# The order in which the two feed-forwards stream a product's moving columns: plain, or every 2nd, 4th, 8th or 16th group of 16 columns first

## The reference, cut to what matters

```python
# first block, layers l = 0, 1: widths 1024 -> 4096 -> 1024
f = jnp.square(jax.nn.relu(x @ mlp_w1[l])) @ mlp_w2[l]
x = _layernorm(DEEPNORM_ALPHA * x + f, ln2_g[l], ln2_b[l])

# second block, layers l = 0, 1: widths 1024 -> 2 * 2816, 2816 -> 1024
up = _dwconv(u @ w_up[l], ffn_conv_w[l], ffn_conv_b[l])
a_half, v_half = jnp.split(up, 2, axis=-1)
h = h + (jax.nn.silu(a_half) * v_half) @ w_down[l]
```

## Time and profile before

| what | value |
|---|---|
| median of 3 runs | 2493.92 us (2493.91 to 2503.79) |
| span of the profiled execution, first to last instruction | 2488.1 us |
| TensorE matmul busy | 2442.7 us, 98%, 17296 instructions |
| TensorE weight load busy | 2242.2 us, 90% |
| VectorE, ScalarE, GpSimd busy | 72%, 58%, 12% |
| HBM traffic over the span | 172 GB/s |
| chain that ended last | TensorE 91%, VectorE 6%, ScalarE 2%, DMA 1% |

### The profile page before, as it was taken

How to read it: one execution, slowest core, us unless ns; L and a number is a source line. 1 busy time by engine, 2 the same in 40 slices (tenths; PEclk the granted TensorE clock), 3 DMA queues, 4 the chain that set the end, 5 groups by cost and what they waited for, 6 DMA issues and landing times.

```text
span 2488.1 us, 42214 instructions
## 1 busy us (share of the span) xinstructions
PE 2442.7 (98%) x17296; PEld 2242.2 (90%) x17296; DVE 1787.2 (72%) x2889; ACT 1450.6 (58%) x2130; POOL 287.8 (12%) x222
## 2 busy tenths in 40 slices
PE   8999999999999999899999999999999999999998
PEld 8888999888889899799999799998899999899996
DVE  5567675565586755678778887885598678887875
ACT  5547555445465554477665655664767656656654
POOL 0000002000000000002123720000012207500000
PEclk9999999999999999999999999999999999999999
DMA  7544576655545566554566645666554567645663
GB/s 257 157 138 119 158 248 199 202 180 164 139 118 153 182 191 203 166 156 125 144 199 189 195 139 185 195 202 191 145 153 136 150 194 203 183 146 190 190 210 127
DMA packets 358917, 430.45 MB, mean 173 GB/s; under 512 B 20616, under 2 KB 286310, under 8 KB 358468
## 3 DMA queue, kind: packets, MB, share of 16 engines
q1 hardware_dynamic: 341312, 401.72, 52.9%
q10 hardware_dynamic: 14340, 14.93, 2.5%
q0 software_dynamic: 3072, 11.10, 1.4%
HBM read 424.44 MB, written 3.24 MB: 172 GB/s over the span
## 4 chain that ended last, share of the span: by engine, by line
PE 91%; DVE 6%; ACT 2%; DMA 1%; issue 1%; ACTq 0%; POOL 0%; POOLq 0%; DVEq 0%
PE ps L112 89%; PE ps L115 2%; DVE wlo L121 1%; DVE sE L121 1%; ACT lnv L118 0%; DMA kT<-in_diff_lambda 0%; DVE sbc L130 0%; DVE sE L124 0%; DVE kT L121 0%; DVE sz L130 0%; DMA mxb<-spread 0%; DMA memN<-in_mem 0%; DVE ys L130 0%; DVE xN L130 0%; ACT L118 0%
## 5 line engine op out<-in xcount | busy, mean ns | idle before, releaser
L121 DVE TENSOR_TENSOR wlo<-wring,whi 128x1024 fp32r<-128x1024 f32 (+1 forms) x768 | 919.3, 1217 | 250.6 <-ACT whi L118 249.8
L118 ACT ACTIVATE whi<-wring 128x1024 fp32r<-128x1024 f32 (+1 forms) x768 | 804.0, 1054 | 428.1 <-PE ps L112 414.7
L112 PE MATMUL ps<-uT,whi 128*128 128x256 f32 x4640 | 816.7, 280 | 6.3 <-DVE wlo L121 5.0
L112 PEld LDWEIGHTS ps<-uT,whi 128*128 128x128 f32 x4640 | 704.0, 188 | 14.8 <-DVE wlo L121 8.2
L112 PE MATMUL ps<-uT,wlo 128*128 128x256 f32 x2320 | 645.2, 278 | 0.0
L112 PEld LDWEIGHTS ps<-uT,wlo 128*128 128x128 f32 x2320 | 437.9, 189 | 0.0
L112 PE MATMUL ps<-xT,whi 128*128 128x256 f32 x2112 | 373.9, 281 | 2.9 <-DVE xT L121 1.7
L112 PEld LDWEIGHTS ps<-xT,whi 128*128 128x128 f32 x2112 | 320.5, 188 | 9.3 <-issue 5.6
L112 PE MATMUL ps<-xT,wlo 128*128 128x256 f32 x1056 | 293.4, 278 | 0.0
L112 PE MATMUL ps<-whi,hid 128*128 128x512 f32 x864 | 269.5, 391 | 0.0
L112 PEld LDWEIGHTS ps<-xT,wlo 128*128 128x128 f32 x1056 | 198.0, 188 | 0.1
(11 more groups left out here) (400 smaller groups left out, 3616.9 us busy)
## 6 DMA issues: line engine op xcount, KB each, us to landing
wring<-in_w_in SPq DMA_DIRECT2D x346, 512.0 KB, 4.0
wring<-in_mlp_w SPq DMA_DIRECT2D x128, 512.0 KB, 4.4
wring<-in_w_up SPq DMA_DIRECT2D x88, 512.0 KB, 4.5
wring<-in_w_down SPq DMA_DIRECT2D x44, 512.0 KB, 4.3
wring<-in_w_branch SPq DMA_DIRECT2D x32, 512.0 KB, 3.4
wring<-in_w_out SPq DMA_DIRECT2D x32, 512.0 KB, 4.3
wring<-in_mem_w_kv SPq DMA_DIRECT2D x16, 512.0 KB, 6.2
wring<-in_w_br_hg SPq DMA_DIRECT2D x16, 512.0 KB, 4.8
```

What stands on the lines that cost most here:

```text
L112: return self.e.matmul(*p, **k) if self.e else Nothing()
L118: return self.e.activation(*p, **k) if self.e else Nothing()
L121: return self.e.tensor_tensor(*p, **k) if self.e else Nothing()
```

## The change

Both forms get a number `n`. Where it is not 0, the moving operand and the output are viewed as groups of 16 columns (64 bytes) and walked with each n-th group first: group 0, n, 2n, ..., then 1, n + 1, ..., with the same walk on both sides, so that every value lands where it did. The weights' side is as before. In the first block's feed-forward n is 2 in layer 0 and 4 in layer 1, in the second block's 8 and 16.

```diff
-                do("tokens", p, x, us, k0_ + k0, first and k0 == 0, fin and k0 + nk == chunks)
+                do("tokens", p, x, us, k0_ + k0, first and k0 == 0, fin and k0 + nk == chunks, rows)
...
-                do("features", p, x, u, k0, chunks)
+                do("features", p, x, u, k0, chunks, rows)
...
-                weave((projB(w1, q * 1024, 1024, xT1, out_h(hid), 0, AB), 1), (rows, 0.4))
+                weave((projB(w1, q * 1024, 1024, xT1, out_h(hid), 0, AB, 4 if l else 2), 1), (rows, 0.4))
...
-                run(projA(w2, 0, 1024, hid, out, (q - 1) * 1024, banks=banks, first=q == 1, fin=q == 4))
+                run(projA(w2, 0, 1024, hid, out, (q - 1) * 1024, banks=banks, first=q == 1, fin=q == 4, rows=4 if l else 2))
...
-            run(projB(a["w_up_2"][l], k0 * 128, 256, uT, out_a(k0)))
-            run(projB(a["w_up_2"][l], DFF2 + k0 * 128, 256, uT, out_v(k0)))
-        down = projA(a["w_down_2"][l], 0, 1024, hid, add_to_h(("h2", l)))
+            run(projB(a["w_up_2"][l], k0 * 128, 256, uT, out_a(k0), rows=16 if l else 8))
+            run(projB(a["w_up_2"][l], DFF2 + k0 * 128, 256, uT, out_v(k0), rows=16 if l else 8))
+        down = projA(a["w_down_2"][l], 0, 1024, hid, add_to_h(("h2", l)), rows=16 if l else 8)
...
+    def rows(x, n):
+
+        return x.rearrange("p (b a s) -> p a b s", a=n, s=16)
...
+                ch, cl = p.hi[:, k, :], p.lo[:, k, :]
+                if n:
+                    ch, cl, o = rows(ch, n), rows(cl, n), rows(us[t].ap[:, 0:p.nb], n)
+                e.matmul(o, xh, ch, start=first and k == 0, stop=False)
+                e.matmul(o, xh, cl, start=False, stop=False)
+                m = e.matmul(o, xl, ch, start=False, stop=fin and k == p.nk - 1)
...
+                if n:
+                    xh, xl, o = rows(xh, n), rows(xl, n), rows(u.ap[0:w, 2 * j0:2 * j0 + 256], n)
```

More of the change, by code:

```diff
@@ L437, in panel, with projA @@
         return p
-    def projA(w, c0, n, x, out, r0=0, k0_=0, banks=None, first=True, fin=True):
+    def projA(w, c0, n, x, out, r0=0, k0_=0, banks=None, first=True, fin=True, rows=0):
         chunks = x.n // 512
@@ L456, in projA, with projB @@
                 yield
-    def projB(w, c0, n, x, out, r0=0, ring=PB):
+    def projB(w, c0, n, x, out, r0=0, ring=PB, rows=0):
         chunks = x.n // 512
@@ L1397, in bank_free, with tokens @@
             e.wait_ge(*at(u.before))
-    def tokens(p, x, us, q0, first, fin):
+    def rows(x, n):
+        return x.rearrange("p (b a s) -> p a b s", a=n, s=16)
+    def tokens(p, x, us, q0, first, fin, n=0):
         e.wait_ge(*at(("lo", p.i)))
@@ L1407, in tokens, with features @@
                 xh, xl = x.at(q0 + k, t * 128, 128)
-                e.matmul(o, xh, p.hi[:, k, :], start=first and k == 0, stop=False)
-                e.matmul(o, xh, p.lo[:, k, :], start=False, stop=False)
-                m = e.matmul(o, xl, p.hi[:, k, :], start=False, stop=fin and k == p.nk - 1)
+                ch, cl = p.hi[:, k, :], p.lo[:, k, :]
[4 more added lines that the diff above has]
+                m = e.matmul(o, xl, ch, start=False, stop=fin and k == p.nk - 1)
             m.then_inc(*up("pe_panel", ("panel", p.i, t)))
-    def features(p, x, u, q0, chunks):
+    def features(p, x, u, q0, chunks, n=0):
         e.wait_ge(*at(("lo", p.i)))
```

## The result

The change made the kernel slower by about one per cent: 2524.7 us, the median of 4 runs (2523.4 to 2528.4), against 2496.1 us for the kernel before beside it (2493.9 to 2503.8). The ratio is 1.0109, with a 95% interval of 1.0090 to 1.0129. That lies within the forecast range and outside the likeliest case, which was no change.

The account below looks back on a forecast made before the run. The prediction took TensorE's row of matmuls to bound the kernel. Profiled span 2488.1 + 0 us for the walks, with the 5.8 us by which the median stands above it, gave 2494 us, range 2464 to 2526 us.

Parts of the forecast that it names:

- the likeliest case: Whole kernel: no effect that can be measured, 2494 us, own range 2487 to 2504 us; chance 0.43.
- What bounds the kernel: Whole kernel: TensorE, busy for 98% of the span; time depends on the distance between matmul starts.
- the pipeline's other side: Feed-forwards: ScalarE and VectorE could follow if PE got faster by all of 30.5 us; a slower PE nothing would hide.
- The counts: Feed-forwards: 2592 matmuls of 256 columns and 1296 of 512 are walked; the last layer's up product, 1056, stays plain.
- the middle of three bounds: Walked matmuls: each row costs a fixed step whatever the order, so the walk adds 0 us.
- The bounds: Walked matmuls: from 30.5 us gained, the loss per row gone, to 30.5 us lost, that loss doubled.
- The worst case: Walked matmuls: each jump, reading or writing, costs another step, 30.5 us slower, 2524 us; this or worse, chance 0.12.
- every changed kind rises by 5.7 or 10.7 to 13.1 ns: Sign in the walked feed-forward matmuls' distances that would show a step paid per jump.
- The weight load in the way: Rival, walked matmuls: moving operand and next weights' streams meet, 17.1 us slower, 2511 us; chance 0.24.
- most at n = 2: Sign of the weight load in the way: distances of 118 ns and durations of 281, most at n = 2.
- Neighbouring rows clash, some n separates them: Rival, walked matmuls: successive rows share a piece of memory; 30.5 us faster, 2463 us, or 10 to 20; chance 0.21.
- The test of right and wrong: Wrong if first block's layers part by over 2 us or any 256-column kind moves by over 2.4 ns.

Follow-up runs that it names:

- e6_narrow: Change with other group sizes, second block's up products keeping 32 of 128 stationary columns, down products reading spaced runs; 2502.0 us against 2501.2 for the kernel before.
- e10_groups_of_64: The change with groups of 64 columns in place of 16; 2493.0 us against 2495.2 for the kernel before, ratio 0.9993.
- e3_even: Kernel before, plain order, with the arena's base moved by 64 bytes; 2551.4 us against 2492.6, one run each.
- e4_places: Second block's feed-forward, plain or walked, panels read 0 to 3 places further on, layer 1 with 64 or 32 stationary columns; 2516.0 us against 2504.6 for the kernel before.
- e12_eights_all_even: All 256- and 512-column products walked in groups of 8 by 4th, operands placed at d = 0; 2485.3 us against 2500.1 for the kernel before, ratio 0.9946.
- read-only kernel: The change with the walk on the moving operand alone, outputs plain; 2524.6 us against 2501.2 for the kernel before, ratio 1.0101.

## Why the prediction was right or wrong

**What bounds the kernel: right.** PE was the bound and stayed it; the whole difference in span (35.0 us) is PE's (34.6 us). The other engines only wait longer for PE, so the paragraph on the pipeline's other side wasn't needed.

**The counts: right.** The part that the change leaves in plain order, 1056 matmuls, stayed at 113.6 ns.

**The step that failed** is the middle of three bounds: "If a row costs its step because the reader hands over a row at a time, the order makes no difference, and the sum is 0. I take 0." It was measured at +28.9 us. Of the reason given the size stands, one step of 0.42 ns for each 64 bytes in plain order. But a fixed time per row doesn't explain it: the walks read the same rows and take longer. The argument went from how even the loss is in plain order to how it would be in another, and plain order is one pattern: it reads through all places of 256 bytes in turn. Rows of one pattern, however many, couldn't tell a fixed cost from one that depends on the pattern. And the loss was not even in the rows at hand: 118.0 ns in the earlier trace rows and 228.8 against 226.4 in the earlier trace rows are the same plain order, and the prediction used them for a rival alone.

**The bounds: right by luck.** The worst case, "each jump costs as much again as each row now loses", gave +30.5 us and 2524 us, and 2524.7 was measured. Its size was near since most of the walks pay about one more step per 16 columns; the 6.3 to 8.1 ns at 256 columns are over its 5.7, and 4.7 and 4.9 at 512 far under its 10.7 to 13.1. Its mechanism was wrong: 64 jumps per matmul cost nothing when the groups are 4 by 4th and the weights narrow (e6_narrow), and groups of 64 cost nothing (e10_groups_of_64). By its own sign, "every changed kind rises by 5.7 or 10.7 to 13.1 ns", the 512-column walks by 4th and 8th fall out at 4.7 and 4.9. The write side cost nothing measurable here: ratio 1.0001 (0.9986 to 1.0017) with runs of 64 bytes. The Trainium skill warns of outputs that aren't contiguous ("PSUM — Partial Sum Buffer", "Specifications (TRN2)"); these runs of 64 bytes don't bear it out.

**The weight load in the way: half right.** That the two operands' streams meet is real, and larger than priced: a shift by 64 bytes costs the kernel before 59 us (e3_even), and at 256 columns narrower weights take that loss away (e4_places). Its price of 17.1 us, from the second distance, missed the walks, which are at 120.0 to 121.7 and not at 118.0 ns; and most of their loss stays with 32 stationary columns: all of it for n = 8, 6.7 of 8.0 ns for n = 2, 4.4 of 6.7 for n = 4. So it isn't the main part of what made the change slower. The forecast's sign "most at n = 2" is there, weakly (121.7 against 120.0).

**Neighbouring rows clash, some n separates them: wrong in sign** for the change's walks. No walk at full rate came under 113.3 ns at 256 columns. That some walk beats plain order is true only of finer groups at another place (e12_eights_all_even).

**The test of right and wrong** worked: kinds of 256 columns moved by 6.3 to 8.1 ns, where the prediction set 2.4 as the point from which it would be wrong. The Trainium skill gives columns over 2.4 GHz plus about 2.5 ns ("TensorE: Matmul & The Clock Gate", "Back-to-back issue gap"), an estimate of 109.2 ns at 256 columns. No row of fp32r matmuls met it: the lowest took 113.3.

What stays open is the law of the walks. For groups of 16 a walk costs if its successive rows keep to one or two of the four 64-byte places (by 8th each place comes twice in a row), and reading through all four (plain, groups of 64) doesn't. But 16-column runs at a step of 48, which go through all four places in reverse, still took 117.6 ns with 32 stationary columns, and 8 by 4th, which keeps to two, is free at d = 0. None of the theories on record fits all the rows.

## What to carry to other kernels

Where TensorE is the bound with rows of short matmuls, take the distance between starts as a thing to measure for each address and order of the operands; moving all buffers by 64 bytes cost 2.4% here (59 of 2493 us, one run each), moving the panels alone 1.6% (four runs), and the best walk gave back 0.5%. Leave the moving operand contiguous, or in pieces of at least 256 bytes; walks of single 64-byte pieces cost up to a step per 16 columns here, while the pattern of the output was free. And an even cost seen in one pattern only is no evidence that the cost is fixed: ask for a row with another pattern, and without one leave the chance of no change lower.

## What the runs showed of the hardware that was not expected

- **The places of the two operands within 256 bytes** set the distance in plain order: at d = 0, 1, 2 and 3 it is 119.9, 113.3 (or 118), 118.7 and 117.8 ns for 256 columns, and with 64 stationary columns instead of 128 the 119.9 falls to 113.4. The Trainium skill says that TensorE has reading ports of its own ("SBUF — State Buffer", "Terms"); these rows don't show another engine in the way, but TensorE's own two streams do meet.
- **Narrow pieces.** Groups of 2 columns (8 bytes) by 2nd take 230.9 ns, half the rate, groups of 4 (16 bytes) by 4th 113.4, the full rate. The Trainium skill's page ("SBUF — State Buffer", "Specifications (TRN2)") says that two hits in each line of 16 bytes give the full bandwidth. Two float32 columns in a row, if they are its two hits, don't get it here: groups of 2 took 164.6 ns (by 64th) to 232.3 (by 4th). Four in a row can. And 4 by 16th at 133.8 ns shows that 16 bytes aren't enough in each order. All of these are with 32 stationary columns.
- **The second distance of 118 ns** comes and goes in the same code, in the feed-forwards too: the last up product in plain order took 113.6 ns in the trace after and 117.8 in the read-only kernel's, and e4_places changed from one to the other within a product. One such layer is 1056 x 4.2 = 4.4 us. How much of the scatter of the runs it makes is not shown: with e12_eights_all_even, where it is gone too, the runs still lie 6 us apart.
- **The granted clock** halves for single stretches, of 3.4 or 7 to 14 us, 30 us in all in the execution of before and 38 in that of after. Such a stretch costs half of its length where TensorE is busy in it, 1.6 us of the 3.4 at 53.4 us, so it moves a row's mean without any change in the code (118.6 ns in place of 113.5 in before's layer 1).
